# Expert weights in 8 KB runs with paired gathers, merge output to logits by tiles, three high slots

## The chip, the cores and the metric

The kernel runs on one core of one Trainium2 chip. The metric is the device time of one execution in microseconds. Unless another type is named, all data is 32-bit floating point (f32); fp32r is the same 32 bits read by TensorE in a rounded form that it multiplies in one pass.

## What is computed

Two blocks in a row on 512 tokens of width 1024. The first block is two layers of a mixer (latent attention beside a convolution), a cross attention to a memory of 256 tokens, and a gated feed-forward stage. The second block is a mixer (windowed attention beside retention), and then a mixture of 64 experts, of which each token uses 2. The change touches mostly the experts and what leads to them:

```python
def hybrid_mixer_2(xn, ...):
    ...
    merged = (g_att * jnp.einsum('bse,ed->bsd', y_att, w_attn_branch)
              + g_ret * jnp.einsum('bse,ed->bsd', y_ret, w_ret_branch))
    return jnp.einsum('bsd,de->bse', merged, w_out)

def hierarchical_moe(x2, w_group, b_group, w_expert, b_expert, w1, w3, w2):
    group_p = jax.nn.softmax(xf @ w_group + b_group, axis=-1)
    g_w, g_idx = lax.top_k(group_p, 1)
    ...
    def expert_block(args):
        xb, e = args
        hid = jax.nn.silu(xb @ w1[e]) * (xb @ w3[e])
        return hid @ w2[e]
    ...

    h = h + mix
    hn = rms_norm_2(h, norm_moe_w[l])
    ffn = hierarchical_moe(hn.reshape(B * S, D), ...)
    h = h + ffn.reshape(B, S, D)
    return rms_norm_2(h, norm_final_w)
```

An expert's w1 and w3 are 1024 x 512, its w2 is 512 x 1024: 2 MB each, 6.29 MB for an expert, 403 MB for all.

## The kernel before

Five programs run side by side, one for an engine (`tensor`, `scalar`, `vector`, `gpsimd`, `sync`, lines 2603 to 2662), and wait for each other by semaphores. Each runs its own list in the order in which it is written; nothing is reordered. Tokens lie in four tiles of 128.

**Weights.** All weights come in pieces of at most 1 MB (`pieces`, line 447), in one fixed order, by DMAs on SP's queue (`load_piece`, line 531). A piece goes into a slot of the on-chip memory; the slots form a ring. A slot is given back when TensorE has used its piece (`release`, line 592), and SP, which works in order, waits for that before it issues the load that uses the slot again. Before the experts the ring has 4 slots (`piece_slots`). Before the expert loop more are added (`add_slot`): `memT`, six `more_slot`s, two in `xT`, two in `piece_high`, which makes 15.

**Split weights.** Most matmuls before the experts are done in fp32r, three for one: high x high, high x low, low x high. ScalarE writes the rounded high part of a piece into one of 2 high slots (`split_high`, line 539), VectorE leaves the rest in the piece itself (`split_low`, line 547). Both do this for piece n+1 at the place in their lists where piece n is named (`act_piece`, `dve_piece`). High slot and piece are free again when TensorE has used the piece.

**Output projections.** `project_out_pe` (line 704) takes 4 or 6 pieces, half of them for output columns 0 to 511 and half for 512 to 1023, 4 token tiles each. With `turned`, the last two pieces are both held, and the tiles are finished one after another (0 and 1, then 2, then 3), so that the norm on VectorE (`project_out_dve`, line 736) can follow tile by tile. The last output of the mixer (`merge_out`) is done without `turned`: piece by piece, four tiles each.

**Router.** After `merge_out` each tile goes through the RMS norm: a square with sum on ScalarE (`square_act`), a power on GpSimd (`root_pool`), a scaling on VectorE (`rms_dve`, line 1583) into `hn`; then TensorE transposes it (`rows_to_T_pe_f32`) and ScalarE copies it to `xT`. ScalarE takes tile i+1 after the copies of tile i. When all four are there, TensorE makes the logits, VectorE picks groups and experts, TensorE counts ranks, VectorE works out the slots of all tokens, and the first `chosen` matrix (which of 512 tokens goes to which of an expert's 64 places) is made.

**Expert loop** (`experts_pe`, line 2402). For each expert n: `gather_pe` multiplies `chosen` with `hn` in f32 (8 matmuls, each 64 columns of `chosen` against 512 columns of `hn`, two at a time in the two halves of the array), `hidden_pe` of expert n-1 (16 f32 pairs for w1 and w3, over four pieces), `rows_T_pe` (4 transposes), `out_pe` of expert n-2 (w2, two pieces), `hidden_T_pe`. ScalarE and VectorE copy between; ScalarE stores each expert's 64 rows (256 KB) to memory. A row of w1 or w3 is 2 KB long, one of w2 is 4 KB long; partition p of a piece takes rows p, p+128 and so on. An expert with more than 64 tokens is handled by a branch (`further`), which is not taken with this data. `combine` fetches the rows, adds them, and does the last norm.

## Time and profile before

| | us |
|---|---|
| median of 3 runs | 3804.83 |
| lowest, highest | 3804.68, 3805.06 |
| the profiled execution | 3806.16 |
| its span in the trace | 3804.3 |

| stretch (us from the span's start) | what |
|---|---|
| 0 to 1847 | first block, two layers |
| 1847 to 2608 | attention, retention, merge |
| 2608 to 2654 | merge output (`merge_out`) |
| 2654 to 2729 | router |
| 2729 to 3766 | experts |
| 3766 to 3804 | combine |

How to read it: the page gives, for 40 equal slices, how busy each engine was, how busy the 16 DMA engines were and how many GB/s they moved. The other views name, for a stretch of time, single instructions with their start, their length and what ended the idle time before them, or the busy time of all engines in chosen windows. A DMA share of 1.04 means that the packets on the 16 engines overlap a little: they are never idle. The granted clock is given as a share of TensorE's full speed, 1.00 for 2.4 GHz and 0.50 for 1.2 GHz.

### The profile page before, as it was taken

Reading aid. Unit: us, or ns where it says so; the run is one execution under the profiler, and the core shown is the slowest. Engines: PE = TensorE matmul, PEld = TensorE weight load, DVE = VectorE, ACT = ScalarE, POOL = GpSimd, SP = SyncE. Lnnn points to the kernel's source line nnn. Section 1 sums busy time; section 2 is a strip of 40 time slices with the busy share of each in tenths; the row PEclk is TensorE's granted clock in tenths of the full one; section 3 lists DMA queues with packets and bytes.
Section 4 is the critical chain, followed back from the end, with each engine's and each line's share of the span. In section 5 each row is a group of like instructions: output and inputs, shape, how many; then the busy total and the mean of one; then the engine's idle time right before and its main releaser. Section 6 shows DMA issues by size and latency. Waiting matters only on the chain.

```text
span 3804.3 us, 36621 instructions
## 1 busy us (share of the span) xinstructions
PE 3398.7 (89%) x15488; PEld 2203.6 (58%) x15488; DVE 1310.1 (34%) x2363; ACT 869.4 (23%) x1371; POOL 153.7 (4%) x142
## 2 busy tenths in 40 slices
PE   5878989999877999999899999898599999999994
PEld 4537668887535667888688877676333333333331
DVE  3375353334266444333534443632311111111112
ACT  2331222222233122222233342121111111111111
POOL 0010000000010000000100100000000000000001
PEclk8989999999988999999999999899699999999997
DMA  4102212323201212233211322033399999999996
GB/s 142 34 1 89 99 56 89 105 80 126 67 1 56 100 62 83 94 100 102 82 60 51 95 72 72 17 100 111 144 393 405 405 407 406 406 406 405 407 404 245
DMA packets 340601, 625.48 MB, mean 164 GB/s; under 512 B 15792, under 2 KB 129200, under 8 KB 340432
## 3 DMA queue, kind: packets, MB, share of 16 engines
q1 hardware_dynamic: 317904, 579.37, 41.5%
q10 hardware_dynamic: 20336, 35.58, 2.6%
q0 software_dynamic: 2192, 8.13, 0.8%
q8 instruction: 124, 2.03, 0.2%
q14 instruction: 45, 0.37, 0.0%
HBM read 600.23 MB, written 22.81 MB: 164 GB/s over the span
## 4 chain that ended last, share of the span: by engine, by line
PE 68%; DVE 10%; DMA 9%; SPq 6%; ACT 3%; POOL 2%; issue 2%; ACTq 0%; DVEq 0%; POOLq 0%
PE bank L121 66%; SPq L163 6%; DMA more_slot<-in_moe_w 4%; PE bank L124 3%; DMA piece<-in_moe_w 2%; DVE gate_acc L139 2%; POOL root L136 1%; DMA piece_high<-in_moe_w 1%; DMA xT<-in_moe_w 1%; DVE x_tok L139 1%; DMA memT<-in_moe_w 1%; DVE stat L154 1%; DVE probs L142 1%; POOL raw_q L136 1%; ACT probs L127 0%
## 5 line engine op out<-in xcount | busy, mean ns | idle before, releaser
L136 DVE TENSOR_TENSOR piece_rounded<-piece,piece_high_rounded 128x2048 fp32r<-128x2048 f32 (+1 forms) x156 | 343.0, 2199 | 680.5 <-ACT piece_high_rounded L127 680.4
L121 PE MATMUL bank<-xT_rounded,piece_high_rounded 128*128 128x512 f32 (+1 forms) x1376 | 542.3, 394 | 29.2 <-DVE piece_rounded L136 14.6
L121 PE MATMUL bank<-xT_low_rounded,piece_high_rounded 128*128 128x512 f32 (+1 forms) x1376 | 532.9, 387 | 0.0
L121 PE MATMUL bank<-xT_rounded,piece_rounded 128*128 128x512 f32 (+1 forms) x1376 | 532.7, 387 | 0.0
L127 ACT ACTIVATE piece_high_rounded<-piece 128x2048 fp32r<-128x2048 f32 (+1 forms) x156 | 283.6, 1821 | 330.3 <-PE bank L121 322.9
L136 DVE TENSOR_TENSOR hids<-silus,bank 64x512 f32<-64x512 f32 x64 | 44.1, 690 | 889.2 <-ACT silus L127 889.2
L121 PEld LDWEIGHTS bank<-xT_rounded,piece_high_rounded 128*128 128x128 f32 x1376 | 262.0, 190 | 87.5 <-DVE piece_rounded L136 15.0
L121 PEld LDWEIGHTS bank<-xT_low_rounded,piece_high_rounded 128*128 128x128 f32 x1376 | 262.0, 190 | 54.4 <-issue 3.8
L121 PEld LDWEIGHTS bank<-xT_rounded,piece_rounded 128*128 128x128 f32 x1376 | 261.7, 190 | 52.2
L121 PE MATMUL bank<-piece,xeT 128*64 128x512 f32 x560 | 246.0, 600 | 15.7 <-DMA more_slot<-in_moe_w 5.5
L121 PE MATMUL bank<-more_slot,xeT 128*64 128x512 f32 x824 | 243.1, 596 | 13.8 <-DMA more_slot<-in_moe_w 7.5
L121 PE MATMUL bank<-hn,chosen 128*64 128x512 f32 x1024 | 235.3, 602 | 17.5 <-DVE chosen L133 17.5
L121 PE MATMUL bank<-piece_high_rounded,xT_rounded 128*128 128x192 f32 (+1 forms) x448 | 150.4, 336 | 19.5 <-issue 16.6
L139 DVE SCALAR_TENSOR_TENSOR gate_acc<-hT,cols,gate_acc 128x512 f32<-128x512 f32 x240 | 163.7, 742 | 0.0
L121 PEld LDWEIGHTS bank<-more_slot,xeT 128*64 128x64 f32 x824 | 80.2, 137 | 127.7 <-issue 127.7
L121 PE MATMUL bank<-piece_high_rounded,hidT_rounded 128*128 128x512 f32 x352 | 139.4, 396 | 9.0 <-DVE hidT_low_rounded L136 9.0
L121 PE MATMUL bank<-piece_rounded,xT_rounded 128*128 128x192 f32 (+1 forms) x448 | 146.8, 328 | 0.0
L121 PE MATMUL bank<-piece_high_rounded,xT_low_rounded 128*128 128x192 f32 (+1 forms) x448 | 146.7, 327 | 0.0
L121 PEld LDWEIGHTS bank<-hn,chosen 128*64 128x64 f32 x1024 | 68.2, 137 | 132.9 <-issue 110.7
L127 ACT ACTIVATE silus<-bank 64x512 f32<-64x512 f32 x64 | 37.8, 591 | 464.7 <-PE bank L121 464.7
L121 PE MATMUL bank<-piece_high_rounded,hidT_low_rounded 128*128 128x512 f32 x352 | 138.5, 394 | 0.0
L121 PE MATMUL bank<-piece_rounded,hidT_rounded 128*128 128x512 f32 x352 | 138.4, 393 | 0.0
(319 smaller groups left out, 4862.4 us busy)
## 6 DMA issues: line engine op xcount, KB each, us to landing
more_slot<-in_moe_w SPq DMA_DIRECT2D x154, 1024.0 KB, 15.2
piece<-in_moe_w SPq DMA_DIRECT2D x104, 1024.0 KB, 15.1
xT<-in_moe_w SPq DMA_DIRECT2D x50, 1024.0 KB, 14.9
piece_high<-in_moe_w SPq DMA_DIRECT2D x50, 1024.0 KB, 15.1
piece<-in_ffn_w_in SPq DMA_DIRECT2D x40, 1024.0 KB, 5.2
memT<-in_moe_w SPq DMA_DIRECT2D x26, 1024.0 KB, 14.9
piece<-in_w_in SPq DMA_DIRECT2D x20, 1024.0 KB, 5.0
piece<-in_xa_w_kv SPq DMA_DIRECT2D x16, 1024.0 KB, 5.3
```

Source lines behind the costliest of these rows:

```text
L121: return self.engine.matmul(*a, **k) if self.engine is not None else Nothing()
L124: return self.engine.transpose(*a, **k) if self.engine is not None else Nothing()
L127: return self.engine.activation(*a, **k) if self.engine is not None else Nothing()
L136: return self.engine.tensor_tensor(*a, **k) if self.engine is not None else Nothing()
L139: return self.engine.scalar_tensor_tensor(*a, **k) if self.engine is not None else Nothing()
L142: return self.engine.tensor_tensor_reduce(*a, **k) if self.engine is not None else Nothing()
L154: return self.engine.bn_stats(*a, **k) if self.engine is not None else Nothing()
L163: return self.engine.dma_start(*a, **k) if self.engine is not None else Nothing()
```

## The change

Four changes in one:

1. **Runs of 8 KB.** Partition p of an expert's weights now takes 8 (w1, w3) or 4 (w2) rows that follow each other in memory, 16 KB in all; each of the two pieces takes half of them, 8 KB in one run. The activations are laid out to match: `rms_dve` writes the norm's columns in another order (`apart`, reading with a stride of 8), and `hidden_dve` reads with a stride of 4.
2. **Gathers for two experts at once.** `gather_pe` runs for every second expert, with all 128 columns of `chosen` for the pair. `hn` is split into fp32r halves (`hn_high` by ScalarE, `hn_low` by GpSimd), and each gather is 16 matmuls of 128x512 in fp32r. 0 and 1 in `chosen` are exact. Rows are transposed 8 at a time for the pair.
3. **Merge output to logits by tiles.** `merge_out` is done with `turned`, and the norm, transposes and logits of a tile follow it. The loads of the router's tables and of the norm's gain are issued earlier.
4. **Three high slots, three piece slots** (before 2 and 4). In the projections the last piece's place in the lists of ScalarE and VectorE is moved ahead of the adds of the second half, so the next weight piece is split before the norms and not between the transposed tiles.

The slots of the expert loop's ring are now 13: three `piece`, `memT`, `y_att_slot`, two `mT_slot`, three `piece_high`, two in `xT`, and `norm_room` (the former `gain` and `shift`). `memT` and `y_att_slot` are filled already during `merge_out`.

```diff
-        self.piece_slots = [self.sb_twin(f"piece{i}", [P, SLOT]) for i in range(4)]
-        self.high_slots = [self.sb_twin(f"piece_high{i}", [P, SLOT]) for i in range(2)]
+        self.piece_slots = [self.sb_twin(f"piece{i}", [P, SLOT]) for i in range(3)]
+        self.high_slots = [self.sb_twin(f"piece_high{i}", [P, SLOT]) for i in range(3)]
...
+        self.early_slots = [self.memT[:, :, :].rearrange("p k s -> p (k s)"), carve("y_att_slot", SLOT)]
+        self.late_slots = [carve(f"mT_slot{n}", SLOT) for n in range(2)] + self.high_slots
...
             for name in ("moe_w1_2", "moe_w3_2", "moe_w2_2"):
-                w = a[name][0, ex]
-                by_rows(name, w, 0, w.shape[0] // P, 0, w.shape[1], wants_split=False, step=SLOT // w.shape[1])
+                for part in range(2):
+                    plan.append((name, self.together(a[name][0, ex], part), False))
...
+    def together(self, w, part):
+        t = w.shape[0] // P
+        return w.rearrange("(p t) n -> p t n", p=P)[:, part * t // 2:(part + 1) * t // 2, :]
...
-        before = self.split_rank[n] - 2
+        before = self.split_rank[n] - 3
...
-        starts = list(range(0, kt, SLOT // BANK))
-        for half in range(2):
-            for k0 in starts[:-1] if half and normed else starts:
-                self.dve_piece(e, label)
-            for i in range(NT if not (half and normed) else 0):
-                self.add_dve(e, key, half, i, scale, x_from, normed)
-        for i in range(NT if normed else 0):
-            self.add_dve(e, key, 1, i, scale, x_from, True)
-            self.norm_dve(e, key, i)
+        pieces = 2 * len(range(0, kt, SLOT // BANK))
+        first = max(pieces // 2, 3 if normed else 0)
+        for _ in range(first):
+            self.dve_piece(e, label)
+        for i in range(NT):
+            self.add_dve(e, key, 0, i, scale, x_from, normed)
+        for _ in range(pieces - first):
+            self.dve_piece(e, label)
+        for i in range(NT):
+            self.add_dve(e, key, 1, i, scale, x_from, normed)
+            if normed:
+                self.norm_dve(e, key, i)
             if after:
                 after(i)
...
+        def turned(i):
+            for n, slot in enumerate(self.early_slots):
+                self.add_slot(f"early{n}", slot, "pe", "m_branch", "retention", KD - 1)
+            for j in (0, 1):
+                self.rows_to_T_pe_f32(e, j)
+
         self.project_out_pe(e, "merge_out", "mixer out", KD,
                             lambda k, i: (self.mT[:, k, i * P:(i + 1) * P], self.mT_low[:, k, i * P:(i + 1) * P]),
-                            [("m_split", c) for c in range(KD)])
+                            [("m_split", c) for c in range(KD)], turned)
...
         for i in range(NT):
-            self.square_act(e, i, self.hn[:, i, :], "moe_norm", ("merge_out", "added", 1, i),
-                            ("merge_out", "summed", 1, NT - 1))
-            ...
+            self.square_act(e, i, self.hn_high[:, i, :], "moe_norm", ("merge_out", "added", 1, i))
+            if i:
+                self.hn_turned_act(e, i - 1)
+        self.hn_turned_act(e, NT - 1)
+        for i in range(NT):
+            self.high_of(e, self.hn_high[:, i, :], self.hn_low[:, i, :]).then_inc(*e.tick("hn_high", i))
...
-        for i in range(NT):
-            for half in range(2):
-                ins = e.matmul(bank[half * CAP:(half + 1) * CAP, :], ch[:, i, :],
-                               self.hn[:, i, half * BANK:(half + 1) * BANK], start=(i == 0), stop=(i == NT - 1))
+        for half in range(2):
+            ...
+            for i in range(NT):
+                for part, hn in enumerate((self.hn_high, self.hn_low)):
+                    ins = e.matmul(bank[:, :], self.rounded(ch[:, i, :, :].rearrange("p a c -> p (a c)")),
+                                   self.rounded(hn[:, i, half * BANK:(half + 1) * BANK]),
+                                   start=(i == 0 and part == 0), stop=(i == NT - 1 and part == 1))
```

**Place 1: TensorE from the end of the merge output to the ranks.** In these rows `mT` is the merged output, `hn` and `hn_low` the normed rows, `router_w` the weights of the logits, `both` the picked experts. Before:

```order
L121 MATMUL bank<-piece_rounded,mT_rounded 128x512
L121 MATMUL bank<-piece_high_rounded,mT_low_rounded 128x512
L124 MATMUL bank<-ident,hn 128x128 x32
L121 MATMUL bank<-router_w,xT 128x72 x32
L121 MATMUL bank<-both,tri 128x64
```

After, at the end of tile 2 and at the end of tile 3:

```order
L120 MATMUL bank<-piece_high_rounded,mT_low_rounded 128x512
L123 MATMUL bank<-ident,hn_low 128x128 x16
L120 MATMUL bank<-piece_high_rounded,mT_rounded 128x512
...
L120 MATMUL bank<-piece_high_rounded,mT_low_rounded 128x512
L123 MATMUL bank<-ident,hn_low 128x128 x8
L120 MATMUL bank<-router_w,xT 128x72 x8
L123 MATMUL bank<-ident,hn_low 128x128 x8
L120 MATMUL bank<-router_w,xT 128x72 x24
L120 MATMUL bank<-both,tri 128x64
```

The transposes of tiles 0 and 1 moved ahead of tile 3's matmuls, and the logits of tile 0 ahead of the transposes of tile 3.

**Place 2: SP's loads from the merge output's weights to the first slot that is used again.** Before:

```order
L163 DMA piece<-in_w_out 128x4x512 x4
L163 DMA piece<-in_moe_w_2 128x4x512 x4
L163 DMA memT<-in_moe_w_2 128x2x1024
L163 DMA more_slot_226<-in_moe_w_2 128x2x1024
L163 DMA more_slot_227<-in_moe_w_2 128x4x512
L163 DMA more_slot_228<-in_moe_w_2 128x4x512
L163 DMA more_slot_229<-in_moe_w_2 128x4x512
L163 DMA more_slot_230<-in_moe_w_2 128x4x512
L163 DMA more_slot_231<-in_moe_w_2 128x2x1024
L163 DMA xT<-in_moe_w_2 128x2x1024
L163 DMA xT<-in_moe_w_2 128x4x512
L163 DMA piece_high<-in_moe_w_2 128x4x512 x2
```

After:

```order
L162 DMA piece<-in_w_out 128x4x512 x4
L162 DMA piece<-in_moe_w_2 128x2048
L162 DMA memT<-in_moe_w_2 128x2048
L162 DMA y_att_slot<-in_moe_w_2 128x2048
L162 DMA piece<-in_moe_w_2 128x2048 x2
L162 DMA mT_slot_230<-in_moe_w_2 128x2048
L162 DMA mT_slot_231<-in_moe_w_2 128x2048
L162 DMA piece_high<-in_moe_w_2 128x2048 x3
L162 DMA xT<-in_moe_w_2 128x2048 x2
L162 DMA norm_room<-in_moe_w_2 128x2048
```

Each load is now one run of 2048 elements for a partition (before four runs of 512 or two of 1024), and 13 loads stand before a slot's second use, where 15 stood.

**Place 3: TensorE at the first two experts.** `rows` are the gathered rows, `xeT` their transposes. Before:

```order
L121 MATMUL bank<-hn,chosen_211 64x512 x8
L124 MATMUL bank<-ident,rows_213 128x128 x4
L121 MATMUL bank<-hn,chosen_212 64x512 x8
L121 MATMUL bank<-piece,xeT_215 64x512 x16
L124 MATMUL bank<-ident,rows_214 128x128 x4
L124 MATMUL bank<-ident,hids_219 128x64 x4
```

After, the last two of the 16 matmuls of the first gather, and what follows:

```order
L120 MATMUL bank<-hn_high_rounded,chosen_rounded 128x512
L120 MATMUL bank<-hn_low_rounded,chosen_rounded 128x512
L123 MATMUL bank<-ident,rows_225 128x128 x8
L120 MATMUL bank<-piece,xeT_227 64x512
L120 MATMUL bank<-y_att_slot,xeT_227 64x512
```

The second expert's gather is gone from ahead of the first expert's hidden matmuls; one gather of 16 single-pass matmuls serves both.

## Rows read from the trace of the kernel before

**Rows 1.** The page's 40 slices: DMA share in tenths, and GB/s.

```profile
DMA  4102212323201212233211322033399999999996
GB/s 142 34 1 89 99 56 89 105 80 126 67 1 56 100 62 83 94 100 102 82 60 51 95 72 72 17 100 111 144 393 405 405 407 406 406 406 405 407 404 245
```

**Rows 2.** Windows: stretch, length, busy us (instructions) by engine, clock, DMA share, GB/s.

```profile
700.00:800.00 100.00, 100.00 (x443) 82.84 (x442) 30.75 (x25) 22.69 (x20) 0.00 (x0) 1.00 0.29 93
2800.00:2900.00 100.00, 100.00 (x482) 34.27 (x478) 14.22 (x42) 13.61 (x25) 0.00 (x0) 1.00 1.04 407
3600.00:3700.00 100.00, 93.34 (x442) 33.94 (x444) 12.18 (x36) 13.02 (x24) 0.00 (x0) 1.00 1.04 405
```

**Rows 3.** Chain that ended last, expert loop: start us, length us, what.

```profile
2870.75 10.45 PE bank L121 x48
2885.76 10.45 PE bank L121 x48
...
2935.58 7.09 PE bank L121 x32
...
3746.29 12.11 PE bank L121 x48
```

**Rows 4.** Windows, as rows 2, in the first cycles after the ring was full.

```profile
2772.00:2776.00 4.00, 4.00 (x20) 1.14 (x16) 0.00 (x0) 0.00 (x0) 0.00 (x0) 1.00 1.03 421
2776.00:2782.00 6.00, 6.00 (x34) 2.33 (x34) 2.03 (x6) 1.19 (x2) 0.00 (x0) 1.00 1.04 408
2788.00:2792.00 4.00, 4.00 (x22) 1.44 (x20) 0.20 (x1) 0.59 (x1) 0.00 (x0) 1.00 1.03 413
...
2814.00:2819.00 5.00, 5.00 (x26) 1.72 (x24) 0.00 (x0) 0.60 (x1) 0.00 (x0) 1.00 1.05 406
2820.00:2825.00 5.00, 5.00 (x26) 1.62 (x22) 2.03 (x6) 0.59 (x1) 0.00 (x0) 1.00 1.04 414
2836.00:2841.00 5.00, 5.00 (x28) 2.00 (x28) 2.03 (x6) 1.19 (x2) 0.00 (x0) 1.00 1.04 420
```

**Rows 5.** SP's queue in order of time: start, length, line, load.

```profile
2747.84 2.12 SPq L163 DMA_DIRECT2D piece<-in_moe_w  x4
2761.15 2.18 SPq L163 DMA_DIRECT2D more_slot<-in_moe_w  x4
2765.32 0.37 SPq L163 DMA_DIRECT2D memT<-in_moe_w  x1
```

**Rows 6.** Timelines of VectorE, ScalarE and TensorE, merge output to first expert.

```profile
2654.14 0.69 DVE L139 SCALAR_TENSOR_TENSOR x_tok<-x_tok,bank 128x512 f32<-128x512 f32 x1 [2.03 <-PE bank L121]
2661.93 1.28 DVE L139 SCALAR_TENSOR_TENSOR hn<-x_tok,root,gain 128x1024 f32<-128x1024 f32 x1 [0.67 <-POOL root L136]
...
2659.93 1.06 ACT L127 ACTIVATE hn<-x_tok 128x1024 f32<-128x1024 f32 x1 [25.58 <-issue]
...
2683.61 13.90 PE L121 MATMUL bank<-router_w,xT 128*128 128x72 f32 x64 [0.78 <-ACT xT L127]
...
2729.41 5.08 PE L121 MATMUL bank<-hn,chosen 128*64 128x512 f32 x16 [15.19 <-DVE chosen L133]
...
2740.77 4.46 PE L121 MATMUL bank<-piece,xeT 128*64 128x512 f32 x20
```

**Rows 7.** TensorE in the loop: all gathers (page's part 5), and one wait.

```profile
L121 PE MATMUL bank<-hn,chosen 128*64 128x512 f32 x1024 | 235.3, 602 | 17.5 <-DVE chosen L133 17.5
...
3002.04 1.08 PE L121 MATMUL bank<-xT,xeT 128*64 128x512 f32 x1 [2.81 <-DMA piece<-in_moe_w]
```

**Rows 8.** VectorE and TensorE between cross attention and feed-forward, layer 0.

```profile
555.19 2.28 DVE L136 TENSOR_TENSOR piece_rounded<-piece,piece_high_rounded 128x2048 fp32r<-128x2048 f32 x1
...
557.62 0.55 PE L121 MATMUL bank<-xT_rounded,piece_high_rounded 128*128 128x256 f32 x1 [7.29 <-DVE piece_rounded L136]
```

**Rows 9.** Unit costs: a GpSimd multiply, and a VectorE add with strided output.

```profile
L136 POOL TENSOR_TENSOR raws<-raws,cos_a 128x512 f32<-128x512 f32 x24 | 31.1, 1296 | 266.3 <-PE bank L121 266.3
...
2602.93 1.06 DVE L136 TENSOR_TENSOR mT_low<-merge_gates,merge_gates 128x512 f32<-128x512 f32 x1
```

More of the change, by code:

```diff
@@ L1275, in cross_pe, with project_out_act @@
             self.rows_to_T_pe(e, f"xT_cross{l}", i, self.x_tok, f"cross{l}", "normed", i)
[L1277 to L1279 removed]
+    def project_out_act(self, e, label, kt):
+        for _ in range(2 * len(range(0, kt, SLOT // BANK))):
             self.act_piece(e, label)
@@ L2243, in router_dve @@
         at = self.at
-        for i in range(NT):
-            self.rms_dve(e, i, self.hn[:, i, :], self.gain[:, :], "moe_norm", ("moe_norm", "gain"))
         W = GROUPS + EXPERTS
@@ L2372, in hidden_pe, with rows_T_pe @@
+    def rows_T_pe(self, e, q):
+        for half in range(2):
+            bank = self.banks.take(e, "xeT", q, half)
+            e.wait_ge(*self.at("rows", q, half))
+            self.transposes(e, bank, [self.rows[q % 2][:, half * BANK + j * P:half * BANK + (j + 1) * P] for j in range(4)]
+                            ).then_inc(*e.tick("pe", "xeT", q, half))
+            self.banks.give(("xeT", q, half), "xeT", q, half)
     def hidden_pe(self, e, n, wg, wu):
-        bank, x = self.banks.take(e, "hidden", n), self.xeT[n % 2]
@@ L2374, in hidden_pe @@
-        e.wait_ge(*self.at("xeT", n))
+        bank, x = self.banks.take(e, "hidden", n), self.xeT[n // 2 % 2]
+        for half in range(2):
+            e.wait_ge(*self.at("xeT", n // 2, half))
         for k in range(KD):
             for part, w in ((0, wg), (1, wu)):
-                ins = e.matmul(bank[part * CAP:(part + 1) * CAP, :], x[:, k % 4, k // 4, :], w[k // 4][:, k % 4, :],
+                ins = e.matmul(bank[part * CAP:(part + 1) * CAP, :], x[:, k, n % 2, :], w[k // 4][:, k % 4, :],
```

239 lines of the change are left out of this document (125 added, 114 removed).

## The prediction, made before the changed kernel was run

> **What bounds the kernel now.** I read the page's slices first. Until slice 29 the DMA engines are busy two or three tenths of the time, and from there to the end of the experts over nine tenths, at 404 to 407 GB/s [rows 1]. So there are two kernels in one: 2740 us in which TensorE sets the pace, and 1005 us of experts. The windows say which resource ends last in the second: at 2800 to 2900 us TensorE is busy for all 100 us and DMA share is 1.04; at 3600 to 3700 us TensorE is busy for 93.3 of 100 us, and DMA share is still 1.04 [rows 2]. The chain confirms it. Early on it runs through TensorE alone, with an expert each 15.01 us (2885.76 - 2870.75). Later it goes through a DMA's landing once for each expert: expert 13's hidden matmuls start at 2935.58 and those of expert 63, the last, at 3746.29, that is 50 experts in 810.7 us, 16.21 us each [rows 3]. TensorE needs 15.0, so weights bound the loop by 1.2 us for an expert, and a change of TensorE alone would return nothing there. An expert moves 6.29 MB of weights and 0.26 MB of stores: 6.55 MB in 16.21 us is 404 GB/s, the page's figure. TensorE's own limit lasts only while the 15 full slots are eaten up; DMA is never idle then either, so what counts for the end is when DMA resumes and how long it then takes.
>
> DMA resumes when the first expert's hidden matmuls give back their slots, at 2747.84 [rows 5]. By then 15 of 384 pieces are on the chip, and 369 (61.5 experts) remain: 61.5 x 16.21 = 997 us, which ends at 2747.8 + 997 = 3745, where the chain has the last wait end. The sum of the change is therefore three terms: what comes before the experts, the shift of this resume, and the DMA time after it. Behind the last weights stands a tail of 3804.3 - 3746.3 = 58 us, which the change leaves as it is but for a strided read of 0.4 us.
>
> **Runs of 8 KB.** What a longer run is worth can be read in the first cycles, since w1 and w3 have 2 KB rows and w2 has 4 KB rows. Loads 16 to 19 are issued at 2747.84, 20 to 23 at 2761.15, load 24 at 2765.32 [rows 5]; loads 23 and 24 are a w2, and at 1 MB in 2.6 us they fall at 2772 to 2776. This returns every 16 us. In four such stretches the rate is 421, 413, 414 and 420 GB/s, mean 417; in two stretches of w1 and w3 without a store it is 408 and 406, mean 407 [rows 4]. For each of 16 engines a 2 KB packet thus takes 2048 x 16 / 407000 us = 80.5 ns and a 4 KB packet 157.2 ns. The second 2 KB cost 76.7 ns, so 3.8 ns belong to the packet itself. An 8 KB packet, which no row shows, comes to 80.5 + 3 x 76.7 = 310.6 ns, 422 GB/s. Bounds: no gain beyond a 4 KB run, or none at all, below; above, 430 GB/s, if 8 KB gains over 4 KB as much as 4 KB over 2 KB, and a little more. For an expert: w1 and w3 take 4.19 MB / 407 = 10.31 us, w2 2.10 / 417 = 5.03 us, together 15.34; the other 0.87 us of 16.21 are stores and their disturbance, and stay. After: 6.29 / 422 = 14.91, + 0.87 = 15.78 us. The ring holds 13 pieces at the resume in place of 15, so 371 pieces or 61.83 experts remain: 61.83 x 15.78 = 976 us against 997, **-21 us**. Two fewer slots cost 5 us of it. They don't starve the DMA engines: when an expert's hidden matmuls start, 4 + 2 slots hold pieces in use, and 7 are left for loads, 18 us of DMA work.
>
> The rows show a gain from 2 to 4 KB. The Trainium skill ("DMA: Bandwidth & Descriptors", Specifications) puts the minimum transfer for line rate at 512 B, by which 2 KB rows would be at line rate already and this term would be +5 us in place of -21. The trace's 407 against 417 speaks against that; it stays a rival.
>
> **Paired gathers.** A gather takes 235.3 us / 64 = 3.68 us of TensorE now [rows 7]. The new one is 16 fp32r matmuls of 128x512 for two experts; such matmuls run 443 in 100 us in the feed-forward stage [rows 2], 0.226 us each, so 3.6 us for the pair and 1.9 us less for each expert. TensorE comes to 2 x 15.0 - 3.7 = 26.3 us for a pair against 31.6 of DMA. Its wait grows from 1.2 to 2.6 us, **0 us** on the path. The longer waits may cost clock: after 2.81 us of waiting four matmul pairs ran at 1.08 us, half speed, where they take 0.59 otherwise [rows 7], 1.7 us lost. Two such dips for a pair make 29.7 us, still under 31.6. Splitting `hn` costs ScalarE four passes of 1.1 us and GpSimd four of 2 x 1.3 us [rows 9], 15 us behind the last transpose, while VectorE and TensorE work 32 us on the ranks; hidden.
>
> **Merge output to logits by tiles.** Now: last add at 2654.14; ScalarE starts the first square only at 2659.93, because it issues the router's DMAs first; then four tiles in turn of 5.9 us; logits from 2683.61 for 13.9 us, to 2697.5; then 31.9 us until the first gather at 2729.41, hidden matmuls at 2740.77, and slots back 7.1 us later [rows 3, 6]. After: the tiles end at about 2640.5, 2643, 2648.7 (TensorE gives 2.72 us to a tile and a piece). Add, square, power and scaling take 4.5 us for a tile, with the scaling 0.7 us longer for its stride (a strided add takes 1.06 us where a plain one takes 0.69 [rows 9]). Tile 1 is normed by 2650, so TensorE waits at most 1 to 2 us for it, transposes tiles 0 and 1, and ends tile 3 at 2657. Its norm is there at 2661.5, its copies in `xT` at 2664.5, and with three tiles' logits done or under way the last end at 2667 (full clock) to 2673 (3.5 us for each tile's logits, as now). Take 2669: 28 us earlier. The ranks take 32 us as before. The first gather runs 16 matmuls, 4 to 7 us, and then transposes of 8 rows; but the second gather, 3.6 us, no longer stands between it and the hidden matmuls. These start 7.5 us after the gather in place of 11.4. Resume at 2716 in place of 2748, **-32 us** (between -26 and -36). Loads don't spoil it: 13 slots are filled by about 2685.
>
> **Three high slots, three piece slots.** Where cross attention meets feed-forward, TensorE stands 7.29 us and starts 0.2 us after VectorE's split of the next piece (2.28 us at 555.19), which sits between the norms and the last transposes' low parts [rows 8]. Moved ahead of the norms it no longer ends that wait, but the norms then start after it: the piece lands 5 us after its slot is free, and ScalarE and VectorE take 4.3 us more, 1.2 us later than the first half tile. Net -1 us, twice; nothing elsewhere. A ring of three is enough, as a piece feeds TensorE for 10.6 us and takes 5 to land. **-2 us** (-5 to +5).
>
> **Sum.** -2 - 32 - 21 = -55 us against 3806.2 of the profiled execution, 3751. The median lies 1.3 us lower, 3804.8, so the forecast is **3750**.
>
> **Rivals.**
> 1. The run length changes nothing (the stretches of w2 are quick because stores fall elsewhere). For it: some stretches of w2 are only 413. Against: all four exceed both of the others. Time: 61.83 x 16.21 = 1002, +5 in place of -21: 3776.
> 2. Longer runs give more, up to 430 GB/s: 14.63 + 0.87 = 15.5, 958 us, -39; with -4 and -36 in the others 3726.
> 3. Slower: the new layout slows the reads. Before, the 128 partitions of a load read one closed stretch, 2 KB after 2 KB; after, each partition starts 16 KB behind the last one, and 16 engines walk in step. If such starts meet in the same part of the memory, the rate falls. Place: each load of the loop. It costs more than the earlier resume returns when an expert's period exceeds (997 + 34) / 61.83 = 16.67 us, weights at 398 GB/s; at 380 it is 17.43 us, 1078 us, and 3852. No load in the trace reads so. The same page of the Trainium skill (Latency and other measured facts) lists a loss for row pitches of 512 KiB and more and names none at 16 KiB; no row here shows it.
> 4. The earlier resume fails, since something else (the split `hn`, the first chosen matrices) holds the first gather: -2 - 21 gives 3782.
>
> **How the numbers follow.** Forecast (3738 to 3765) 0.60; rival 1 0.17; rival 2 0.10; rival 3 0.06; rival 4, or a mixture with slower early stages that still gains, 0.04; gains and losses that cancel 0.03. A measurement of this kernel tells about 0.2%, 7.6 us, from no change. Faster 0.91, same 0.03, slower 0.06. The range takes in rivals 1 and 2 up to 3722 and 3778 and leaves out rival 3 and what exceeds it.
>
> **What would show it.** In the profile after: the rate in the loop at 418 to 422 GB/s in place of 406, DMA share over 1 throughout; hidden matmuls of consecutive experts 15.8 us apart, by pairs; gathers at about 115 us in total; first slots back near 2714 on the trace; logits ending near 2667; cross attention to feed-forward a wait of 6 us. The prediction is wrong if the DMA share falls below 1 in the loop (13 slots too few, or TensorE too slow), if the rate stays at 406, or if the stretch before 2600 us grows by more than 5 us.

## The result, and the profile after

The changed kernel takes 3745.8 us (median of 4 runs, 3739.4 to 3747.4) where the kernel before takes 3804.9 in the same comparison: a ratio of 0.984, 95% interval 0.982 to 0.986, or 59 us less. 3750 was forecast. The profiled execution took 3747.37 us, with a span of 3745.5; it is the slowest of the four.

The total is nearly right, but two of its terms are not, in opposite directions. It pays to read the profile for that.

**The loop.** The page's row of GB/s slices and of packets answers to [rows 1]:

```profile
GB/s 133 35 1 79 112 57 85 100 86 113 92 0 45 101 57 79 94 103 104 76 69 56 81 79 69 29 79 90 162 360 423 422 423 423 423 422 422 423 420 254
DMA packets 225012, 625.41 MB, mean 167 GB/s; under 512 B 14768, under 2 KB 128176, under 8 KB 175696
```

From slice 31 to the end of the experts the same bytes go at 420 to 423 GB/s in place of 404 to 407. One wide window over the loop (TensorE's busy time first; granted clock, DMA share and GB/s last), of before and then of after, answers to [rows 2]:

```profile
2800.00:3600.00 800.00, 761.71 (x3598) 272.04 (x3594) 101.53 (x300) 108.49 (x200) 0.00 (x0) 1.00 1.04 406
```

```profile
2800.00:3600.00 800.00, 727.30 (x3286) 308.71 (x3288) 110.69 (x205) 111.17 (x205) 0.00 (x0) 0.94 1.01 423
```

DMA share is still over 1, and TensorE is busy for 91% of the time where it had 95% over the same window before. The last part of the chain of waits, of after, answers to [rows 3]; it goes through a landing again and again, two experts to a pair:

```profile
3580.03 11.86 PE bank L120 x48
...
3610.99 13.42 PE bank L120 x48
...
3668.85 19.19 DMA piece<-in_moe_w
3688.17 12.23 PE bank L120 x48
3700.42 0.60 ACT outs L126
```

A pair of experts takes 3610.99 - 3580.03 = 30.96 us, an expert 15.5. The windows read 422 or 423 GB/s, taken as 422.5 below, and 6.554 MB at that rate take 15.51 us. The hidden matmuls of the last expert start at 3688.17. So DMA bounds the loop as before, and it does so at 15.5 us where the prediction said 15.78.

**The resume.** SP's loads, which answer to [rows 5]:

```profile
2722.35 0.33 SPq L162 DMA_DIRECT2D piece<-in_moe_w  x1
...
2737.61 0.33 SPq L162 DMA_DIRECT2D mT_slot<-in_moe_w  x1
```

The first slots come back at 2722.35, 25.5 us earlier than before; 32 were forecast. The rows of the router show where the rest is, and answer to [rows 6]. VectorE's last add and scaling, TensorE's transposes and logits, then the logits on VectorE, the first gather and the first hidden matmuls:

```profile
2657.23 0.69 DVE L138 SCALAR_TENSOR_TENSOR x_tok<-x_tok,bank 128x512 f32<-128x512 f32 x1 [1.81 <-PE bank L120]
2657.91 1.90 PE L120 MATMUL bank<-router_w,xT 128*128 128x72 f32 x16
2659.95 2.08 DVE L138 SCALAR_TENSOR_TENSOR hn_low<-x_tok,root,norm_room 128x1024 f32<-128x1024 f32 x1 [0.66 <-POOL root L135]
2662.08 1.97 PE L123 MATMUL bank<-ident,hn_low 128*128 128x128 f32 x8 [2.27 <-DVE hn_low L138]
2663.84 10.36 PE L120 MATMUL bank<-router_w,xT 128*128 128x72 f32 x48
2674.24 0.46 DVE L135 TENSOR_TENSOR logits<-bank,router_b 128x288 f32<-128x288 f32 x1 [12.21 <-PE bank L120]
2706.27 0.80 PE L120 MATMUL bank<-hn_high_rounded,chosen_rounded 128*128 128x512 f32 x1 [15.35 <-DVE chosen_rounded L135]
2715.23 0.61 PE L120 MATMUL bank<-piece,xeT 128*64 128x512 f32 x1 [0.88 <-DVE xeT L129]
```

Tile 0's logits take 1.90 us. Then TensorE waits 2.27 us for the last scaling, and from there on the same work goes at half the speed: three tiles in 10.36 us, 3.45 each. The granted clock is 1.00 over tile 0's logits and 0.50 over the other three. The logits are done at 2674.24; the prediction had 2667 to 2673 and took 2669. The ranks take the 32.0 us they took before (2674.24 to 2706.27), and the gather to the hidden matmuls takes 9.0 us, not 7.5: most of the gather's 16 matmuls follow each other at 0.43 us, the pace of the lower of TensorE's two clock levels (1.2 GHz), and only the last two at 0.24 us. The mean granted clock of these 9.0 us is 0.66.

**Early stages.** At the wait of [rows 8], where cross attention meets feed-forward:

```profile
557.77 0.55 PE L120 MATMUL bank<-xT_rounded,piece_high_rounded 128*128 128x256 f32 x1 [6.07 <-DVE xT_low_rounded L135]
```

7.29 us have become 6.07, as forecast (about 6).

### The profile page after: what moved, and what is told of

It reads as the page before. It is cut to its first block, busy times and chain, and to the rows that moved or that the text cites. A ratio compares the mean times of both kernels' runs of the same rounds, so it can differ in the third digit from the quotient of the medians.

```text
span 3745.5 us, 35516 instructions
## 1 busy us (share of the span) xinstructions
PE 3326.5 (89%) x14976; PEld 2239.5 (60%) x14976; DVE 1323.0 (35%) x2235; ACT 873.1 (23%) x1375; POOL 161.3 (4%) x146
## 4 chain that ended last, share of the span: by engine, by line
PE 67%; DMA 16%; DVE 10%; ACT 3%; POOL 2%; issue 2%; ACTq 0%; DVEq 0%; POOLq 0%
PE bank L120 65%; DMA piece<-in_moe_w 3%; DMA piece_high<-in_moe_w 3%; DMA mT_slot<-in_moe_w 3%; DMA xT<-in_moe_w 2%; PE bank L123 2%; DVE gate_acc L138 2%; DMA norm_room<-in_moe_w 1%; POOL root L135 1%; DMA memT<-in_moe_w 1%; DVE x_tok L138 1%; DMA y_att_slot<-in_moe_w 1%; DVE stat L153 1%; DVE probs L141 1%; POOL raw_q L135 1%
## 5 line engine op out<-in xcount | busy, mean ns | idle before, releaser
L120 PE MATMUL bank<-xT_rounded,piece_high_rounded 128*128 128x512 f32 (+1 forms) x1376 | 543.6, 395 | 25.5 <-DVE xT_low_rounded L135 13.6
L135 DVE TENSOR_TENSOR gate_and_hidden<-gate_and_hidden,bank 64x512 f32<-64x512 f32 x64 | 69.1, 1080 | 844.7 <-ACT gate_and_hidden L126 844.7
L120 PE MATMUL bank<-piece_high,xeT 128*64 128x512 f32 x464 | 184.6, 628 | 15.4 <-DMA piece<-in_moe_w 10.7
L120 PE MATMUL bank<-xT,xeT 128*64 128x512 f32 x312 | 161.6, 666 | 16.3 <-DMA piece_high<-in_moe_w 9.8
L120 PE MATMUL bank<-mT_slot,xeT 128*64 128x512 f32 x304 | 151.0, 652 | 12.1 <-DMA piece_high<-in_moe_w 12.1
L126 ACT ACTIVATE gate_and_hidden<-bank 64x512 f32<-64x512 f32 x64 | 37.8, 590 | 507.4 <-PE bank L120 507.4
L135 POOL TENSOR_TENSOR root<-root,power 128x1 f32<-128x1 f32 (+2 forms) x60 | 61.0, 1016 | 1582.5 <-DVE root L132 1582.5
```

Source lines behind the costliest of these rows:

```text
L120: return self.engine.matmul(*a, **k) if self.engine is not None else Nothing()
L126: return self.engine.activation(*a, **k) if self.engine is not None else Nothing()
L135: return self.engine.tensor_tensor(*a, **k) if self.engine is not None else Nothing()
```

## A mark for comparing profiles

The 2600 us ahead of the experts differ by some us from execution to execution of the same instructions, and the after profile happened to be the slowest of its kind. So the profiles are compared from one common mark: the first matmul of the mixer's output product, which no variant below moves.

```profile
2608.26 0.77 PE L120 MATMUL bank<-piece_high_rounded,mT_rounded 128*128 128x512 f32 x1 [5.84 <-DVE mT_low_rounded L135]
```

It stands at 2608.26 after and 2608.02 before. Counted from it, the loads resume at 139.8 us before (2747.84 - 2608.02) and at 114.1 us after (2722.35 - 2608.26). "From the mark" below means this.

## Experiments on the loop

My theory was that the run length sets the rate of the loads. The rivals were that it doesn't, that only packets of a certain size matter, and that the distance between the runs matters.

**1. Rows as before in the changed kernel.**

```
-    return w.rearrange("(p t) n -> p t n", p=P)[:, part * t // 2:(part + 1) * t // 2, :]
+    half = w[part * rows:(part + 1) * rows, :]
+    return half.rearrange("(q p t) n -> p q t n", p=P, t=run)   # run = 1
```

> The changed kernel with its expert weights read in rows as before (2 KB for w1 and w3, 4 KB for w2), and the activations in the matching order; all else of the change stays. For an expert that is 2560 packets in place of 768, 112 more on each of 16 DMA engines. Theory A, the run length alone sets the rate: the loop falls from 422 back to 406 GB/s, the period of an expert rises from 15.5 to 16.2 us, and 61.8 experts cost 44 us: 3790. Theory B, the prediction's 3.8 ns for a packet holds and the rest of the quicker loop comes from elsewhere (paired gathers, fewer slots): period 15.93 us, +27 us, 3773. Rival 1 of the prediction, run length changes nothing: 3746.

Measured 3797.75 us (10 runs): 52 us more than the changed kernel, more than either theory said. The window shows why:

```profile
2800.00:3600.00 800.00, 705.40 (x3106) 292.78 (x3104) 86.45 (x194) 104.97 (x193) 0.00 (x0) 0.92 1.04 399
```

399 GB/s, less than the 406 of the kernel before with the same rows. So nearly the whole gain of the change hangs on the run length (without it the ratio to before is 0.998), and something else in the change lowers the rate by 7 GB/s. This kernel also gave a by-product. Its scaling is not strided:

```profile
2653.27 1.28 DVE L140 SCALAR_TENSOR_TENSOR hn_low<-x_tok,root,norm_room 128x1024 f32<-128x1024 f32 x1 [0.66 <-POOL root L137]
```

1.28 us where the changed kernel has 2.08 to 2.25, and its logits come 63.5 us from the mark, not 66.0. By this pair of profiles the stride costs 2.5 us on the path.

**2. Runs of 4 KB.** The same edit with run = 2 for w1 and w3, and 1 for w2. As the activations stay in the order of the changed kernel, this kernel's products are not the reference's; it moves the same bytes and runs as many instructions. Experiment 3 is made in the same way.

> The changed kernel with weights in runs of 4 KB (two rows of w1 and w3 together, one of w2): 1536 packets for an expert in place of 768, 48 more on each engine. The activations keep the order of the changed kernel, so the experts' products pair inputs with other rows of the weights than the reference. Theory A (6.3 ns for a packet, what 16.2 against 15.5 us would give): +0.30 us for an expert, +19 us, 3765. Theory B (3.8 ns): +0.18 us, +11 us, 3757. If there is a threshold between 4 and 8 KB or between 2 and 4 KB instead of a price for a packet: 3790 or 3746.

Measured 3767.6 us (3764.5 to 3770.4), 22 us more than the changed kernel. The window:

```profile
2800.00:3600.00 800.00, 719.02 (x3206) 302.47 (x3205) 108.74 (x200) 108.74 (x200) 0.00 (x0) 0.93 1.03 412
```

With 6.554 MB for an expert the three rates of one kernel are three periods: 16.43 us at 399, 15.91 at 412, 15.51 at 422.5. Each engine moves 64 packets fewer for an expert from the first to the second and 48 fewer from the second to the third: 0.52 / 64 = 8.1 ns and 0.40 / 48 = 8.3 ns. The rates are read to half a GB/s, so each price is good to some 0.8 ns. So there is no threshold between 2 and 8 KB: **in the changed kernel each packet costs about 8.2 ns**, over its bytes. The 3.8 ns of the prediction was less than half of that. Both theories priced the packet too low. Experiment 5 shows that the price isn't the same in every kernel.

There is a rival that no run here tests: the price may lie in SP's issuing and not in the packets. Before, SP's queue is never free for long in the loop. Its issues fill 784 of the 800 us of the window, 2.6 us for a load; in the changed kernel they fill 206 us, 0.67 for a load (735 us with rows of 2 KB, 496 with runs of 4 KB). The chain of the kernel before goes through these issues each time, which the "..." of [rows 3] leave out:

```profile
2914.13 7.52 SPq L163
...
2921.69 13.76 DMA memT<-in_moe_w
...
2948.15 5.28 SPq L163
```

Three things speak for the packets. The first four loads of [rows 5], issued when the DMA engines had little to do, took SP 0.53 us each (2.12 / 4), so the rest of the 2.6 us looks like waiting for the loads ahead. And the DMA share is 1.04 before and 1.03 with runs of 4 KB: the engines don't wait for SP. And from 4 to 8 KB the price is the same, though SP is free for 304 and 594 of the 800 us there. That SP's queue is held up by the engines, and not the engines by it, is argued from this and not shown.

**3. Runs of 8 KB closed up.** run = 4, and 2 for w2: the runs of a load start 8 KB apart, not 16.

> The changed kernel with runs of 8 KB as now, but the 128 runs of a load closed up in memory, 8 KB from start to start, where they start 16 KB apart now. As many packets, as many bytes. The activations keep the order of the changed kernel, so the experts' products pair inputs with other rows of the weights than the reference. Theory: the price hangs on packets, not on where they start: no difference, 3746 (within 5). Rival (the mechanism of rival 3 of the prediction, at a smaller size than it needs): starts 16 KB apart cost something now, and closing them gives a higher rate than 422 GB/s and up to 20 us.

Measured 3744.3 us (3742.3 to 3746.5), the same as the changed kernel, at 422 GB/s. Whether the runs start 8 or 16 KB apart makes no difference; the mechanism of the prediction's rival 3 isn't there.

**4. Stores twice.**

```
+            if twice:
+                e.dma_start(self.y_other[n * CAP:(n + 1) * CAP, half * BANK:(half + 1) * BANK], ...)
```

> The changed kernel, each expert's output stored twice, the second time to an array that nothing reads: 0.26 MB more in 128 packets of 2 KB for an expert. Theory A: a store costs its bytes at the loop's rate, 0.26 / 422 = 0.62 us for an expert and 40 us in all, 3785; the prediction's 0.87 us was then too much, and the weights are read at 423 GB/s. Theory B: a store costs 0.87 us as the prediction took it, 54 us in all, 3800, and the weights are read at 430 GB/s. Rival: writes run beside reads at little cost, under 10 us.

Measured 3785.3 us, 39.5 us more. Over 64 experts that is 0.62 us each, and the rate in the window stays at 423 GB/s with the stores counted in. Theory A holds: a store costs its bytes. Of the prediction's remainder of 0.87 us, 0.62 are stores; the other 0.25 us don't belong to the stores, so they were the weights'.

**5. Runs of 8 KB alone in the kernel before.** The same layout, put into the kernel before with nothing else.

> The kernel before with the expert weights in runs of 8 KB (activations in the matching order) and nothing else of the change: gathers by expert, 15 slots, the late router. TensorE needs 15.0 us for an expert there. The prediction's term: period 15.78 us, 61.5 x 0.43 = 26 us less, 3779. Theory A, the run length alone sets the rate (422 GB/s): period 15.5, 40 us less, 3765. Theory B: a packet costs 8.2 ns (16.43, 15.91 and 15.51 us for an expert at 2, 4 and 8 KB in the changed kernel), the kernel before reads rows of 2 KB quicker than the changed one does (406 against 399 GB/s) and keeps that lead: period 16.14 - 0.92 = 15.2 us, 430 GB/s, 56 us less, 3749.

Measured 3765.5 us (3765.1 to 3769.3), a ratio of 0.990 (0.988 to 0.991), 41 us less than before. The window:

```profile
2800.00:3600.00 800.00, 791.21 (x3762) 280.87 (x3760) 126.29 (x312) 113.42 (x209) 0.00 (x0) 1.00 1.01 425
```

425 GB/s, a little more than the changed kernel's 422.5. TensorE is busy for 791 of 800 us here, at full clock, and still doesn't hold the loop back. Theory A's 40 us were right. Theory B's 56 us, which stood on 8.2 ns for a packet, were not: from 406 to 425 GB/s the period falls from 16.14 to 15.42 us, and 0.72 us over the same 112 packets for an engine is 6.4 ns (6.0 by the medians: 41 us, 61.5 experts). So the price of a packet is 6 ns in one kernel and 8 ns in the other. The lead that the kernel before has in rate shrinks from 7 GB/s at 2 KB to 2 or 3 at 8 KB. This one part brings two thirds of the change's 59 us.

**6. Gathers by expert in the changed kernel.**

```
-  ins = e.matmul(bank[:, :], self.rounded(ch[:, i, :, :]...), self.rounded(hn[:, i, half * BANK:...]), ...)
+  ins = e.matmul(bank[half * CAP:(half + 1) * CAP, :], ch[:, i, :], self.hn_low[:, i, half * BANK:...], ...)
```

> The changed kernel with gathers as before: one fp32 gather for each expert out of an unsplit hn, single copies; runs of 8 KB, 13 slots and the earlier router stay. The prediction: pairing is worth 0 on the path, since an expert takes 15.5 us of DMA and 15.0 of TensorE; the resume comes up to 4 us later, as the second gather stands before the first expert's hidden matmuls: 3746 to 3750. Rival: the paired gathers are what lowers the rate of the loads (399 GB/s with rows of 2 KB where before has 406); then the rate rises to 430 GB/s and 18 us are gained, 3730. Second rival: TensorE with its waits no longer keeps up, the period rises above 15.7, 3760 or more.

Measured 3744.3 us (3742.3 to 3750.4), the same as the changed kernel. Its rate is 422 GB/s, so with runs of 8 KB the pairing doesn't lower the rate. With rows of 2 KB, where the 7 GB/s are missing, it wasn't tried. It resumes 116.3 us from the mark (114.1 with pairs), TensorE is busy 785 of 800 us at full clock (727 at a mean of 0.94 with pairs), and none of it reaches the end. The pairing is worth 0, as forecast. So a lower granted clock in the loop costs nothing either, as long as DMA sets the pace.

**7. The kernel before with 13 slots.**

```
-  self.more_slots = [... for n in range((WORK - self.taken) // SLOT)]
+  self.more_slots = [... for n in range((WORK - self.taken) // SLOT - 2)]
```

> The kernel before with 13 slots for the experts' weights in place of 15 (two of the slots in the work room left out), nothing else. Theory A, more loads in flight read faster (7 of 13 slots can be in flight when an expert's matmuls start, 9 of 15): the rate falls from 406 to the 399 GB/s of the changed kernel with rows of 2 KB, 0.29 us for each of 62 experts, and the two missing MB cost 5 us, 23 us in all, 3829. Theory B, the prediction's: two fewer slots cost 5 us and the rate stays, 3811; the difference between 406 and 399 GB/s then lies elsewhere (which addresses the slots have, when the stores fall).

Measured 3818.1 us, 12 us more than before (ratio 1.0021 to 1.0042), between the two theories. The window has 404 GB/s:

```profile
2800.00:3600.00 800.00, 755.12 (x3554) 270.79 (x3550) 99.55 (x294) 106.20 (x196) 0.00 (x0) 0.99 1.04 404
```

From 406 to 404 is 0.08 us for an expert, 5 us, and the two missing MB cost 5. So slots are worth a little more than their MB, but they explain 2 of the 7 GB/s between experiment 1 and the kernel before. The other 5 stay open. The three piece and three high slots aren't the cause: experiment 8 has them, in a ring of 15, and reads rows of 2 KB at 407 GB/s. The addresses of the other slots, the order in which slots come back and paired gathers beside rows of 2 KB weren't tried apart.

## Experiments on the router and the early stages

**8. The early part alone in the kernel before** (three high and three piece slots, and the order of splits and adds).

> The kernel before with three high and three piece slots and the order of splits and adds of the change in the five early product stages, and nothing else of it. The prediction: 2 us less (5 less to 5 more). By the trace of the changed kernel, whose merge begins 0.2 us later than before: 0, 3805. Rival: the early part gained 5 us by 1760 us and something else in the change gave it back in retention; then 3800.

Measured 3805.2 us (10 runs), a ratio of 0.9993, interval 0.9984 to 1.0003: between 6 us less and 1 more. The window over the loop is that of the kernel before:

```profile
2800.00:3600.00 800.00, 762.05 (x3600) 272.17 (x3598) 101.58 (x300) 108.49 (x200) 0.00 (x0) 1.00 1.04 407
```

The mark says more. It stands at 2608.0, 2608.4 and 2607.2 in the three profiles without this part (before, and experiments 5 and 7) and at 2602.7 to 2608.3, mean 2604.9, in the eleven with it: 3 us earlier on average (this variant's own stands at 2606.4). In the after profile a gain of 5 us (a stage that starts at 1759.31 in place of 1764.36) is gone again by the mark; but that profile is at the end of the spread, and read alone it would have said 0.

The loss between the two is real in part. At that stage, the last down product of the feed-forward, the eleven stand at 1756.8 to 1759.3 and the three at 1763.6 to 1764.8, 6.5 us apart on average. From there to the first product of the second block the kernel before takes 82.5 us (1764.36 to 1846.87) and the changed one 85.8 (1759.31 to 1845.07). 2.3 us of these 3.3 are one wait, for the first normed tiles. Before, and then after:

```profile
1824.44 1.97 PE L124 MATMUL bank<-ident,xn_tok 128*128 128x128 f32 x8 [4.72 <-DVE xn_tok L139]
```

```profile
1823.31 1.97 PE L123 MATMUL bank<-ident,xn_tok 128*128 128x128 f32 x8 [7.05 <-DVE xn_tok L138]
```

The norms start later, as the prediction said of the cross attention; it expected nothing of the kind here ("nothing elsewhere").

**9. The late router in the changed kernel.** Norm, transposes and logits only after the last sum, four tiles in turn; the tables still come early.

```
-  self.project_out_dve(..., lambda i: self.rms_dve(e, i, self.hn_low[:, i, :], ...))
+  self.project_out_dve(...)          # the four rms_dve stand at the start of router_dve
```

> The changed kernel with the merge output normed, transposed and multiplied for the router only after its last sum, tile after tile, as before; the tables are still loaded early. Theory: the resume of the loads slips by what the logits slip, up to 25.5 us less the early table loads (some 5 us of it): 20 us, 3766. Rival: the loads' resume isn't what the end hangs on (idle stretches of DMA behind it take the shift up): under 10 us, 3755 or less.

Measured 3758.8 us (3756.8 to 3760.6), 13 us more. The loads resume 128.8 us from the mark, so 14.7 us later than with tiles, and that reaches the end nearly in full. The estimate of 20 was too high: 11.0 of the 25.7 us (139.8 - 128.8) come from what this variant keeps. By its edit that is the tables' issue ahead of the squares, squares that don't wait for the last sum, and one gather less ahead of the first expert (2.2 us by experiment 6); the first two weren't measured apart.

## Experiments towards a faster kernel

**10. Earlier release and a 14th slot.**

```
+            if halfway and k == 3:
+                ins.then_inc(*e.tick("pe", "hidden_half", n))
+                halfway()                 # gives back the first halves of w1 and w3
...
+        self.add_slot("router_room", self.router_slot, "slots", 1)
```

> The changed kernel with more for the loads: the first halves of w1 and w3 go back after half of an expert's hidden matmuls (3.5 us before their end) and that of w2 after half of the output matmuls, and the room of the router's tables (2408 words, dead once the ranks are out) becomes a 14th slot. Theory: the loads resume 3.5 us earlier, the idle 5.7 us between the first and the second refill go, and a 14th MB is there: 2.5 us more; in all 9 to 12 us less than the changed kernel's 3746, 3735. If more loads in flight also read faster, 3 us on top. Rival: the loop's DMA has its own slack elsewhere and only the 14th slot counts, 3743.

Measured 3740.4 us (3736.2 to 3741.7), 5.4 less than the changed kernel; 9 to 12 were expected. SP resumes at 2716.64, 110.7 us from the mark, 3.4 earlier as expected, and the 14th MB is worth 2.5 by its bytes. That makes 5.9, so nothing is left for the rest. The idle stretch behind the resume stays. Windows of 10 us from the resume on, of the changed kernel and then of this one:

```profile
2722.40:2732.40 10.00, 7.85 (x30) 5.15 (x32) 1.94 (x5) 2.12 (x4) 0.00 (x0) 0.83 0.91 355
2732.40:2742.40 10.00, 10.00 (x54) 3.65 (x48) 2.37 (x3) 0.77 (x2) 0.00 (x0) 1.00 0.55 197
```

```profile
2716.60:2726.60 10.00, 7.77 (x32) 4.45 (x28) 1.94 (x5) 1.57 (x3) 0.00 (x0) 0.86 0.89 355
2726.60:2736.60 10.00, 10.00 (x48) 4.24 (x49) 0.64 (x1) 1.19 (x2) 0.00 (x0) 0.97 0.53 197
```

The second refill comes 15.3 us after the first in both, because both moved together. The expectation counted the shift for the first and forgot it for the second. The kernel before has such a stretch too (317 and 276 GB/s in the 20 us behind its resume), so the prediction's "DMA is never idle then" was wrong. By their bytes these 20 us fall short of the loop's rate by 5.4 us before and 6.9 us after, so it cancels but for 1.5 us.

**11. The router's clock.** Logits of tiles 0 and 1 ahead of the last transposes, and 28 matmuls that nothing reads ahead of the first gather.

```
-            if i < 2:
-                self.rows_to_T_pe_f32(e, i + 2)
+            if i in (0, 2):
+                self.rows_to_T_pe_f32(e, 2 + i // 2)
```

> The changed kernel with another order in the router: logits of tiles 0 and 1 before the last tile's transposes (they fill 2.3 us in which TensorE waits, and the clock should stay at its upper level), and 28 matmuls of 128x512 that nothing reads in the 15 us in which TensorE waits for the first chosen matrices. Theory: logits 7 us earlier (1.9 us for a tile in place of 3.45, and one tile done in the wait), the first gather 3.8 us in place of 6.6: the resume is 9 to 10 us earlier, 3736. Rival: the clock stays low whatever fills the wait; then only the tile moved into it, 3.5 us, 3742.

Measured 3741.6 us (3740.2 to 3744.0), 4.2 less than the changed kernel; 9 to 10 were expected. From the mark the loads resume at 111.5 us, 2.6 earlier; the rest of the 4.2 is within the spread. The clock did what the theory said: 32 logit matmuls now take 3.69 us, 1.85 for a tile, and the logits are done 58.4 us from the mark, 7.6 earlier. But VectorE's chain behind them lost most of it at once:

```profile
2661.33 4.66 POOL L135 TENSOR_TENSOR hn_low_rounded<-hn_low,hn_high_rounded 128x1024 fp32r<-128x1024 f32 x2 [4.97 <-ACT hn_high_rounded L126]
```

```profile
2663.19 0.46 DVE L135 TENSOR_TENSOR logits<-bank,router_b 128x288 f32<-128x288 f32 x1 [4.71 <-PE bank L120]
2663.68 0.19 DVE L147 TENSOR_REDUCE v<-logits 128x4 f32<-128x32 f32 x1
2663.90 2.14 DVE L135 TENSOR_TENSOR t<-logits,v 128x32 f32<-128x32 f32 x1
2666.07 2.27 DVE L135 TENSOR_TENSOR t<-t,down 128x32 f32<-128x32 f32 x1
2668.37 0.19 DVE L147 TENSOR_REDUCE v<-t 128x4 f32<-128x32 f32 x1
2668.59 2.04 DVE L135 TENSOR_TENSOR oh_g<-down,v 128x32 f32<-128x32 f32 x1
2670.67 0.19 DVE L135 TENSOR_TENSOR g<-logits,v 128x32 f32<-128x32 f32 x1
```

Three operations on 32 elements take 2.0 to 2.3 us, about the length of one of GpSimd's four passes over `hn` (4.66 us for two), where the same kind takes 0.19 when GpSimd is done. They are those with two inputs in SBUF; the reductions with one input take 0.19 in between. That is 5.9 us of the 7.6. In the changed kernel the passes end (9.29 us from 2665.70) just as the logits come (2674.24), so the split of `hn` was hidden there, as the prediction said, but with no room to spare. The Trainium skill ("SBUF — State Buffer", SBUF: two separate sides) describes this: the port pair of VectorE and GpSimd is an exclusive lock, which a VectorE operation with two SBUF inputs and a GpSimd operation that reads SBUF can't share. The trace agrees, one input against two included. The fillers shortened the first gather's way by 0.9 us only (8.1 in place of 9.0): they end 7.7 us before it, and its first nine matmuls run at the pace of the lower level again.

**12. All of it, and a norm behind the next tile's combination in the last stage.**

```
+            if i:
+                self.rms_dve(e, i - 1, self.results[i - 1], self.last_gain, ...)
```

> Both of these together, and in the last stage each tile's norm put behind the next tile's combination, so that VectorE (4.1 us for a tile) no longer waits for ScalarE and GpSimd (6.5 us from tile to tile): 7 us less behind the last output. Theory: the parts add, 10 + 9 + 7 = 26 us under the changed kernel, 3720. Rival: the parts share their gain, because the ring is then filled later than the loads resume: 3730.

Measured 3727.3 us (3726.8 to 3730.8), a ratio to before of 0.980 (0.978 to 0.981), and 18.5 us less than the changed kernel: 5.4 + 4.2 from the two parts above, and the last stage. There the first fetch to the end of the span is 29.3 us (3695.67 to 3725.0) where the changed kernel needs 34.6 (3710.94 to 3745.5), 5.2 of the 7 expected. The parts come to 14.8 us; the other 3.7 have no cause that the profiles show, and the runs of the changed kernel spread by more. From the mark the loads resume at 108.0 us, 6.1 earlier, which is 3.4 and 2.6 of the two parts. So the parts do not share their gain, and this version beats both kernels.

## Why the prediction was right, term by term

Counted on the two profiled spans, 3804.3 and 3745.5:

| term | forecast | measured | from |
|---|---|---|---|
| early stages, up to the mark | -2 | +0.2 in this pair of profiles, -3 on average | the mark |
| mark to resume | -32 | -25.7 | 139.8 against 114.1 |
| resume to the last expert's hidden matmuls | -21 | -32.6 | 998.45 [rows 3, 5] against 3688.17 - 2722.35 = 965.82 |
| tail | 0 | -0.7 | 58.0 against 57.3 |
| sum | -55 | -58.8 | |

**Runs of 8 KB: the mechanism was right, the term mis-sized.** It came out 12 us larger. The steps that failed are "3.8 ns belong to the packet itself" and the remainder of 0.87 us that was to "stay". The 3.8 ns were read from single stretches of 4 to 6 us [rows 4], which differ by 8 GB/s among themselves, and each of which can hold packets of several loads and of both sizes. Whole kernels of different run length give 8.2 ns in the changed kernel and 6.0 to 6.4 in the one before. The remainder was put down to stores; stores are 0.62 us of it (experiment 4), and the other 0.25 went. The 422 GB/s for the weights after was met, but by luck: the same stretches gave a rate for 2 KB rows that was too high (407, where the loop as a whole, w2 and stores included, has 406) and a price that was too low. The rivals 1 and 3 are refuted by experiments 1 and 3, rival 4 by the resume. Rival 2 had the right period (15.5 us) with 430 GB/s for the weights, but for the wrong reason, a gain beyond a constant price for each packet. The Trainium skill ("DMA: Bandwidth & Descriptors", Specifications) puts the minimum transfer for line rate at 512 B. Read as the prediction read it, as line rate from there on, it doesn't hold here: the changed kernel shows 399 GB/s with rows of 2 KB (4 KB for w2), 412 with runs of 4 KB and 422.5 with 8 KB.

**Two slots fewer: 5 us.** The 5 us for the missing MB were right, but experiment 7 has 12 us at rows of 2 KB, 5 of the other 7 from a slightly lower rate, which the prediction excluded ("they don't starve the DMA engines"), and 2 with no cause named.

**Paired gathers: 0 on the path.** Right, by experiment 6. The two dips in clock that the prediction priced at 1.7 us each are in the trace and harmless.

**Merge output to logits by tiles: right mechanism, 6 us too much.** Of the 6.3 us missing, 5 are in the logits (2674.2 in place of 2669): the prediction named 3.5 us for each tile as its late bound and took a value nearer to the full clock, and the stride costs 2.1 to 2.25 us on each tile's scaling where it had 2.0. The gather's way is 9.0 us in place of 7.5. Most of both comes from TensorE's clock after a wait: at tile 0's 1.9 us the other three tiles would have taken 4.7 us less.

**Three high slots, three piece slots: -2.** Within what can be told: 3 us by the marks, 1 us by the medians. The forecast wait, 6 us, is 6.07. But the sum is right by luck here: 6.5 us are gained up to the last feed-forward, where 2 were forecast, and 3.3 are lost in it, where nothing was (experiment 8).

So the forecast of 3750 rests on one term 12 us too small and one 6 us too large. That it came within 4 us is in part luck; the mechanisms of both terms are those that the runs show. The order of size was wrong as well: the prediction took the router for the largest part; it is the run length (41 us alone in the kernel before, 52 us when it is taken out of the changed one).

## What to carry to other kernels

Where a loop is bound by loads, price a packet and not a threshold: read the period at two run lengths of whole kernels, divide the difference by the packets saved on each engine, and lay the weights' rows together until the rest is small. The price holds for the kernel in which it was read: it was 6 ns in one of these and 8 in the other. Look next at what keeps the loads from resuming after a full ring, since each us of it comes back nearly whole, while time taken from an engine that waits for the loads returns nothing. Before work is moved to an earlier time, see what it will then run beside: the hidden passes on GpSimd were free only while VectorE had no operation with two SBUF inputs.

## What the runs showed of the hardware

- In the changed kernel a DMA packet cost 8.2 ns over its bytes on each of the 16 engines (16.43, 15.91 and 15.51 us for an expert at 2560, 1536 and 768 packets of weights); in the kernel before it cost 6.4 ns (16.14 and 15.42 us at 2560 and 768). By an estimate from the first price 16 KB runs would save another 24 packets an engine, 0.2 us of 15.5; that wasn't tried.
- In the loop SP's queue was held for 2.6 us by the issue of a 1 MB load with rows of 2 KB (784 of 800 us) and for 0.67 us with runs of 8 KB (206 of 800 us).
- The distance between the starts of 8 KB runs, 8 or 16 KB, changed nothing (3744.3 and 3745.8 us).
- The same rows of 2 KB were read at 406 GB/s by the kernel before, 404 with 13 slots, and 399 by the changed kernel; the last step has no cause yet.
- VectorE's operations of 0.19 us with two SBUF inputs took 2.0 to 2.3 us beside GpSimd's passes of 2.3 us, those with one input 0.19.
- TensorE's logits ran at 1.9 us for a tile behind unbroken work and at 3.45 us after a wait of 2.27 us; with the wait filled, all four ran at 1.85.
